# A two-piece fp32 product on TensorE: the high weight piece against two halves into one place, instead of 512 columns into two

## The chip, the cores and the metric

One core of one Trainium2 chip runs the whole program. Times are microseconds (us) of device time. The kernel before was run three times: 2857.05 us median, 2854.23 to 2864.59. The profile is of one further execution.

## The reference, cut to what matters

Two transformer blocks over 256 tokens of width 2048, in fp32. The first has a gated short convolution, a state space mixer (SSD) and attention over a memory, then latent attention (MLA); the second has a retention mixer and an MLP with squared ReLU. What matters here is that nearly all the work is products of the activations with weight matrices in fp32:

```python
h = rms_norm(x, norm0_w);  ... = h @ w_in0 ...;   x = x + y @ w_out0
h = rms_norm(x, norm1_w);  ... = h @ w_in1 ...;   x = x + y @ w_out1
q, k, v, g = split(rmsnorm(x, norm1) @ ret_w_in); ...  x = x + y @ ret_w_out
x = x + square(relu(rmsnorm(x, norm2) @ mlp_w_up)) @ mlp_w_down
return rmsnorm(x, final_norm)
```

## The kernel before, in words

Activations are kept transposed: 128 features on the partitions, T = 256 tokens along the row. To get near fp32 accuracy out of the one-pass fp32r matmul, each value is split in two fp32r pieces. For activations the pieces `m[:, 0]` (high) and `m[:, 1]` (low) lie side by side, 512 columns in all (`hs`, `ys`, `lat`). For a weight tile of 128x128, ScalarE writes the rounded high piece `w_hi` (L403) and VectorE the remainder `w_lo` (L727), eight tiles in one operation of 128x1024. The product wanted is `w_hi*m_hi + w_hi*m_lo + w_lo*m_hi`.

The program goes through phases in a fixed order (`PHASES`): mem, gate, gate_out, ssd, out0, latent, latent_tail, memq, mla, out1, ret_a, ret_out_a, ret_b, ret_out_b, then up and down four times. Each phase is a loop whose body is a row of panels. A panel is up to 16 weight tiles (1 MB of fp32), loaded by SyncE's queue into `raw`, and in most phases gives one output of 128x256. There are 7232 weight tiles in all. In gate_out a panel gives two outputs of 8 tiles each; in out0 and out1 two panels of 10 tiles give one output.

On TensorE a tile is two matmuls (`panel`, L1395 and L1398): `w_hi` against all 512 columns, into both halves of a PSUM bank of `pj`, and `w_lo` against the 256 high columns, into the first half. A bank so gathers two partial sums that have still to be added. VectorE reads only one operand from PSUM here, so ScalarE first copies the first half into `half` (L408, `copy_half`), and VectorE adds the second half to it (L736 or L739, `evac`). Where the output has to be scaled by `rstd`, a second VectorE operation follows (L741). In the phases that add to the residual stream (`residual`), the sum goes to a small tile and a further operation adds it to `xT` (L932); the up phases then need three more operations for the squared ReLU.

`pj` has two banks, so output o may only start once output o-2 has been taken (semaphore `evacuated`). `w_hi` and `w_lo` have four slots of eight tiles: the pieces of panel p+2 overwrite those of panel p, once TensorE has started on the other half of the panel (`half_started`). Each engine works through its own list in written order. On ScalarE this is, per panel j: `split` half 0 of panel j+2, `copy_half` of output j, `split` half 1. On VectorE it is the same with `evac` in the middle. What a phase adds of its own (tanh, softmax, norms) stands between these.

Three further waits will be named. `square_sum` (L1495) is the sum of squares of the new residual stream, which TensorE can only start when VectorE has added up the last output of the phase (L948 is the drain that signals it). `qk_ready` in mla (L1234) comes when VectorE has turned the rotary part, after the outputs 3 and 4 of the body. And the out phases wait for the last rows of `ys` (L748).

Of the kernel before, what the change touches and what calls it, by code (L numbers as in the profile page):

```python
# [25 lines left out]
P = 128  # L26
# [83 lines left out]
def build(nc, streams, w_dt, vecs, consts, mla_mask, ret_tab, ret_decay, pos, x, mem, out):  # L110
    ctx = ExitStack()
    with ctx:
# [14 lines left out]
        kv = sb("kv", [P, 2048])  # L127
        half = sb("half", [P, NB, T])
        wdt = sb("wdt", [P, 16, 32])
# [73 lines left out]
        output_ready = sem("output_ready")  # L203
        half_copied = sem("half_copied")
        evacuated = sem("evacuated")
# [185 lines left out]
        def _(act):  # L391
# [60 lines left out]
            def mem_body(i):  # L452
                for j in range(8):
                    split("mem", i, j, 0)
                    copy_half("mem", i, j)
                    split("mem", i, j, 1)
                    if i == 0 and j < 2:
                        act.wait_ge(S["x_rows"], 16)
                        row_square(1, rows, j)
                        if j == 1:  # L460
                            act.drain().then_inc(S["x_squares"], 1)
                    if i == 0 and j == 2:
                        row_rsqrt(1, "x_var", "x_rsqrt")
                    if i == 1 and j < 4:
                        hi_columns(16 + 2 * j, hs, "norm0")
                        hi_columns(17 + 2 * j, hs, "norm0")
                    if j >= 5:
                        value_rows(i, j - 5)
                value_rows(i, 3)
# [8 lines left out]
            def gate_body(i):  # L478
                for j in range(4):
# [3 lines left out]
                    split("gate", i, j, 0)  # L483
                    copy_half("gate", i, j)
                    split("gate", i, j, 1)
# [8 lines left out]
            def gate_out_body(i):  # L494
                for j in range(4):
                    split("gate_out", i, j, 0)
                    copy_half("gate_out", i, 2 * j)
                    copy_half("gate_out", i, 2 * j + 1)
                    split("gate_out", i, j, 1)
# [4 lines left out]
            def residual(name, ppo):  # L504
# [3 lines left out]
                def body(i):  # L508
                    for j in range(len(PHASES[name][0])):
                        split(name, i, j, 0)  # L510
                        if j % ppo == ppo - 1:
                            o = j // ppo
                            copy_half(name, i, o)
                        split(name, i, j, 1)
# [25 lines left out]
            def ssd_body(i):  # L540
                O = outputs("ssd", i)
                M = Count(0, 1, i)
                for j in range(12):
# [33 lines left out]
                    copy_half("ssd", i, j)  # L577
                    split("ssd", i, j, 1)
# [8 lines left out]
            def copy_body(name):  # L587
                def body(i):
                    for j in range(len(PHASES[name][0])):
                        split(name, i, j, 0)  # L590
                        copy_half(name, i, j)
                        split(name, i, j, 1)
# [6 lines left out]
            for j in range(3):  # L599
# [4 lines left out]
                split("latent_tail", 0, j, 0)  # L604
                copy_half("latent_tail", 0, j)
                split("latent_tail", 0, j, 1)
# [3 lines left out]
            def memq_body(i):  # L610
                O = outputs("memq", i)
                M = Count(4, 2, i)
                for j in range(4):
# [4 lines left out]
                    split("memq", i, j, 0)  # L618
                    copy_half("memq", i, j)
                    if j < 3:  # L620
# [9 lines left out]
            def mla_body(i):  # L630
                O = outputs("mla", i)
                for j in range(8):
# [17 lines left out]
                    if j == 3:  # L650
                        copy_half("mla", i, 3)
                        copy_half("mla", i, 4)
                        split("mla", i, j, 0)
                    elif j == 7:
                        copy_half("mla", i, 8, 2)
                    else:
                        copy_half("mla", i, j if j < 3 else j + 1)
                    split("mla", i, j, 1)
# [7 lines left out]
            def ret_body(name, first):  # L666
                def body(i):
                    O = outputs(name, i)
                    for j in range(12):
# [20 lines left out]
                        split(name, i, j, 0)  # L690
                        copy_half(name, i, j)
                        split(name, i, j, 1)
# [8 lines left out]
            for b in range(FF_BLOCKS):  # L701
                def up_body(i):
                    for j in range(4):
                        split(f"up{b}", i, j, 0)
                        copy_half(f"up{b}", i, j)
                        split(f"up{b}", i, j, 1)
# [10 lines left out]
        def _(dve):  # L717
# [11 lines left out]

            def evac(name, i, o, dst, weight=1, scale=None, via=None):  # L730

                c = outputs(name, i)
                dve.wait_ge(half_copied, c(o, 1))
                k = c.slot(o, NB)
                if scale is None:
                    TT(dst, pj[:, k, T:2 * T], half[:, k], ALU.add).then_inc(evacuated, weight)  # L736
                else:
                    via = dst if via is None else via
                    TT(via, pj[:, k, T:2 * T], half[:, k], ALU.add)  # L739
                    dve.drain()  # L740
                    TT(dst, via, scale, ALU.mult).then_inc(evacuated, weight)  # L741

# [165 lines left out]
            def residual(name, ppo, opp=1, x_all=None):  # L908
# [8 lines left out]
                def body(i):  # L917
                    def column(gain, o):
                        return vec[:, bass.ds(i * 4 + (VEC[gain][0] + o), 1)]
                    for j in range(len(PHASES[name][0])):  # L920
# [194 lines left out]
            def latent_body(i):  # L1115
                for j in range(4):
                    split("latent", i, j, 0)
                    evac("latent", i, j, lraw[:, i * 4 + j], scale=rstd[:, 0:T], via=(krA, krB)[j % 2])
                    split("latent", i, j, 1)
# [225 lines left out]
            inverse_rms(NORM["b_mlp"] + 1, 0, D, nv, ny, nt, rstd, b=258)  # L1345
            TT(rstd_sq, rstd, rstd, ALU.mult)
            for b in range(FF_BLOCKS):
                def up_body(i):
                    for j in range(4):
                        split(f"up{b}", i, j, 0)  # L1350
                        evac(f"up{b}", i, j, up_t[j % 2])
                        split(f"up{b}", i, j, 1)
                        dve.drain()
                        STT(out=up_t[2 + j % 2], in0=up_t[j % 2], scalar=0.0, in1=up_t[j % 2], op0=ALU.max,
                            op1=ALU.mult)
                        dve.drain()
                        TT(up_t[2 + j % 2], up_t[2 + j % 2], rstd_sq[:, 0:T], ALU.mult)
                        yy = ys[:, i * 4 + j]
# [11 lines left out]
        def _(pe):  # L1370
            mm = nc.tensor.matmul

            def panel(name, i, j, pieces, before={}):
# [10 lines left out]
                for o, moving, at, opens, closes, weight in pieces:  # L1384
# [3 lines left out]
                    for t, m in enumerate(moving):  # L1388
# [483 lines left out]
```

## Time and profile before

| | |
|---|---|
| median of the three runs | 2857.05 us |
| span of the profiled execution | 2861.9 us |
| TensorE matmul, busy | 2769.8 us (97%), 15792 matmuls and as many weight loads |
| VectorE busy | 1954.6 us (68%) |
| ScalarE busy | 1405.5 us (49%) |
| DMA | 173 GB/s in the mean, queue q1 busy 49.2% |
| granted TensorE clock | 0.986 in the mean |

The profiled execution took 2861.9 us from its first to its last instruction; this is 4.9 us above the median of the runs shown, within their spread. A matmul's start in the profile is real, its end is modelled, so matmuls overlap on the page: the time of one is read as the distance from its start to the next start. PEld is the weight load, which runs beside the matmul ahead of it. In the chain that ended last, 90% of the span is TensorE's, 56% of the span on line 1395 and 28% on line 1398.

### The profile page before, as it was taken

To read this page: it belongs to the slowest core of one execution; us is meant where nothing else is said; L and a number is where in the kernel's file an instruction comes from. 1 tells how busy PE (TensorE), PEld (TensorE's weight loads), DVE (VectorE), ACT (ScalarE), POOL (GpSimd) and SP (SyncE) were. 2 spreads that over 40 slices of the span, in tenths; PEclk is the share of its full clock that TensorE was granted. 3 is DMA by queue.
4 is the path that set the end of the run, shared out by engine and by line. 5 is a ranking of instruction groups with operands and counts; after the bars stand their busy time and mean duration, and the time that the engine had idled before them with its cause. 6 is when DMAs were issued, how large, how long until landed. Compare 5 with 4: busy or idle time off the path is not lost.

```text
span 2861.9 us, 46279 instructions
## 1 busy us (share of the span) xinstructions
PE 2769.8 (97%) x15792; PEld 2412.3 (84%) x15792; DVE 1954.6 (68%) x3079; ACT 1405.5 (49%) x2199; POOL 35.4 (1%) x56
## 2 busy tenths in 40 slices
PE   6999999999999899999999999999999999999998
PEld 5888888888888788888888888888888888888887
DVE  5566567787767777777666655666667677576775
ACT  5544245555554555556555534555554444444444
POOL 0000000000000001000000000000000000000000
PEclk9999899999999999999999999999999999999999
DMA  5555354444664334465454455454445555555553
GB/s 230 193 190 191 119 193 151 154 147 149 199 226 152 112 128 159 150 194 182 169 179 172 172 176 182 177 179 171 152 166 188 191 189 191 191 191 190 187 188 110
DMA packets 76338, 495.57 MB, mean 173 GB/s; under 512 B 8544, under 2 KB 8672, under 8 KB 23792
## 3 DMA queue, kind: packets, MB, share of 16 engines
q1 hardware_dynamic: 73568, 478.18, 49.2%
q0 software_dynamic: 2000, 13.70, 1.3%
q10 hardware_dynamic: 704, 2.83, 0.3%
q8 instruction: 38, 0.62, 0.1%
q14 instruction: 28, 0.23, 0.0%
HBM read 486.29 MB, written 8.39 MB: 173 GB/s over the span
## 4 chain that ended last, share of the span: by engine, by line
PE 90%; DVE 4%; ACT 2%; issue 2%; DVEq 1%; DMA 0%; ACTq 0%; POOLq 0%
PE pj L1395 56%; PE pj L1398 28%; PE mx L1410 1%; ACT w_hi L403 1%; PE mx L1466 1%; DVE w_lo L727 1%; PE mx L1695 0%; PE mx L1636 0%; DVEq L930 0%; PE mx L1525 0%; PE mx L1637 0%; PE mx L1687 0%; PE mx L1702 0%; DMA xT<-in_mem 0%; PE mx L1513 0%
## 5 line engine op out<-in xcount | busy, mean ns | idle before, releaser
L1395 PE MATMUL pj<-hs,w_hi 128*128 128x512 f32 x4400 | 1562.2, 399 | 6.7 <-DVE xT L741 5.0
L727 DVE TENSOR_TENSOR w_lo<-raw,w_hi 128x1024 fp32r<-128x1024 f32 x1010 | 1137.0, 1130 | 480.6 <-ACT w_hi L403 463.0
L403 ACT ACTIVATE w_hi<-raw 128x1024 fp32r<-128x1024 f32 x1010 | 983.2, 979 | 672.7 <-PE pj L1395 669.2
L1398 PE MATMUL pj<-hs,w_lo 128*128 128x256 f32 x4400 | 1231.2, 280 | 0.0
L1395 PEld LDWEIGHTS pj<-hs,w_hi 128*128 128x128 f32 x4400 | 829.0, 188 | 198.9 <-DVE xT L741 5.3
L1395 PE MATMUL pj<-ys,w_hi 128*128 128x512 f32 x2560 | 906.3, 398 | 20.3 <-DVE ys L748 14.2
L1398 PEld LDWEIGHTS pj<-hs,w_lo 128*128 128x128 f32 x4400 | 833.6, 189 | 3.7 <-issue 2.9
L1398 PE MATMUL pj<-ys,w_lo 128*128 128x256 f32 x2560 | 720.5, 281 | 0.0
L1395 PEld LDWEIGHTS pj<-ys,w_hi 128*128 128x128 f32 x2560 | 483.8, 189 | 136.0 <-DVE ys L748 15.4
L1398 PEld LDWEIGHTS pj<-ys,w_lo 128*128 128x128 f32 x2560 | 487.8, 191 | 0.0
L408 ACT ACTIVATE half<-pj 128x256 f32<-128x256 f32 x491 | 186.9, 381 | 557.5 <-PE pj L1398 556.6
L736 DVE TENSOR_TENSOR gen<-pj,half 128x256 f32<-128x256 f32 x412 | 173.7, 422 | 140.3 <-ACT half L408 134.6
L1395 PE MATMUL pj<-lat,w_hi 128*128 128x512 f32 x272 | 102.2, 415 | 3.9 <-DVE gen L736 2.5
L932 DVE TENSOR_TENSOR xT<-xT,gen 128x256 f32 (+1 forms) x144 | 61.3, 425 | 27.9 <-issue 27.5
L1398 PE MATMUL pj<-lat,w_lo 128*128 128x256 f32 x272 | 76.8, 282 | 0.0
L1395 PEld LDWEIGHTS pj<-lat,w_hi 128*128 128x128 f32 x272 | 51.8, 190 | 20.7 <-issue 5.0
L519 ACT ACTIVATE gen<-xT 128x256 f32 (+1 forms) x64 | 26.8, 418 | 61.6 <-DVE xT L932 61.5
L748 DVE TENSOR_TENSOR ys<-gen,ys 128x256 f32 (+1 forms) x88 | 42.8, 486 | 14.6 <-issue 14.6
L1398 PEld LDWEIGHTS pj<-lat,w_lo 128*128 128x128 f32 x272 | 52.2, 192 | 0.2
L739 DVE TENSOR_TENSOR gen<-pj,half 128x256 f32<-128x256 f32 x59 | 24.9, 423 | 28.1 <-ACT half L408 27.7
L1410 PE MATMUL mx<-con,xT 128*128 128x128 f32 x136 | 22.3, 319 | 21.3 <-DVE xT L785 20.7
L937 DVE TENSOR_TENSOR gen<-gen 128x256 f32<-128x256 f32 x80 | 32.3, 421 | 11.9 <-ACT gen L519 11.9
(262 smaller groups left out, 1356.4 us busy)
## 6 DMA issues: line engine op xcount, KB each, us to landing
raw<-in_w_up SPq DMA_DIRECT2D x64, 1024.0 KB, 4.8
raw<-in_w_down SPq DMA_DIRECT2D x64, 1024.0 KB, 4.8
raw<-in_w_ssd SPq DMA_DIRECT2D x48, 1024.0 KB, 4.8
raw<-in_w_ret_a SPq DMA_DIRECT2D x48, 1024.0 KB, 4.8
raw<-in_w_ret_b SPq DMA_DIRECT2D x48, 1024.0 KB, 4.8
raw<-in_w_out SPq DMA_DIRECT2D x64, 640.0 KB, 3.9
raw<-in_w_gate SPq DMA_DIRECT2D x32, 1024.0 KB, 4.8
raw<-in_w_mem SPq DMA_DIRECT2D x16, 1024.0 KB, 5.0
```

Of the source, the lines that this page charges most:

```text
L403: A(w_hi[:, s, 0:b - a, :], raw[:, c.slot(p, 4), a:b, :], ACT.Copy).then_inc(hi_ready, 1)
L408: A(half[:, c.slot(o, NB)], pj[:, c.slot(o, NB), 0:T], ACT.Copy).then_inc(half_copied, weight)
L519: ins = A(sq[k][o % 2], xT[:, i * 4 + o], ACT.Square, scale=dyn(gain, i, o))
L727: TT(w_lo[:, s, 0:b - a, :], raw[:, c.slot(p, 4), a:b, :], w_hi[:, s, 0:b - a, :].bitcast(F32), ALU.subtract).then_inc(split_ready, 1)
L736: TT(dst, pj[:, k, T:2 * T], half[:, k], ALU.add).then_inc(evacuated, weight)
L748: return TT(dst[1], src, dst[0].bitcast(F32), ALU.subtract)
L932: TT(xo, xo, res[(o + u) % 2], ALU.add).then_inc(S["x_tile"], 1)
L937: TT(acc[k], acc[k], sq[k][o % 2], ALU.add)
L1395: ins = mm(pj[:, k], w_hi[:, s + h, u], m, start=opens and t == 0, stop=False)
L1398: ins = mm(pj[:, k, 0:T], w_lo[:, s + h, u], m[:, 0], start=False, stop=closes and t == len(moving) - 1)
L1410: return nc.tensor.transpose(dst, src, ident)
L1466: ins = mm(mx[:, 0, 32 * r:32 * r + 32], hs[:, k, part, 128 * r:128 * r + 128].bitcast(F32), wdt[:, k], start=k == 0 and part == 0, stop=k ...
```

## The change

A tile is now three matmuls of 256 columns, all into the first half of the bank: `w_hi` against the high columns, `w_hi` against the low columns, `w_lo` against the high columns. PSUM then holds the finished sum. `copy_half` becomes `panel_done`: ScalarE still waits for the output at the same place in its list, and copies nothing. VectorE takes the output in one operation that reads PSUM: a copy (plain outputs), a multiplication by `rstd` (scaled outputs), an addition into `xT` (residual phases), or `max(.,0) * rstd` (up phases). The tile `half` and its semaphore are gone.

```diff
-            def copy_half(name, i, o, weight=1):
-                c = outputs(name, i)
-                act.wait_ge(output_ready, c(o, 1))
-                A(half[:, c.slot(o, NB)], pj[:, c.slot(o, NB), 0:T], ACT.Copy).then_inc(half_copied, weight)
+            def panel_done(name, i, o):
+                act.wait_ge(output_ready, outputs(name, i)(o, 1))
...
-            def evac(name, i, o, dst, weight=1, scale=None, via=None):
+            def product(name, i, o):
                 c = outputs(name, i)
-                dve.wait_ge(half_copied, c(o, 1))
-                k = c.slot(o, NB)
+                dve.wait_ge(output_ready, c(o, 1))
+                return pj[:, c.slot(o, NB), 0:T]
+
+            def evac(name, i, o, dst, weight=1, scale=None):
+                src = product(name, i, o)
                 if scale is None:
-                    TT(dst, pj[:, k, T:2 * T], half[:, k], ALU.add).then_inc(evacuated, weight)
+                    v.tensor_copy(dst, src).then_inc(evacuated, weight)
                 else:
-                    via = dst if via is None else via
-                    TT(via, pj[:, k, T:2 * T], half[:, k], ALU.add)
-                    dve.drain()
-                    TT(dst, via, scale, ALU.mult).then_inc(evacuated, weight)
+                    TT(dst, src, scale, ALU.mult).then_inc(evacuated, weight)
...
                             for u in range(opp):
-                                if u:
-                                    dve.drain()
-                                evac(name, i, o + u, res[(o + u) % 2])
-                                dve.drain()
                                 xo = xT[:, i * n_out + (o + u)]
-                                TT(xo, xo, res[(o + u) % 2], ALU.add).then_inc(S["x_tile"], 1)
+                                TT(xo, xo, product(name, i, o + u), ALU.add).then_inc(evacuated, 1)
+                                dve.drain().then_inc(S["x_tile"], 1)
...
-            TT(rstd_sq, rstd, rstd, ALU.mult)
...
-                        evac(f"up{b}", i, j, up_t[j % 2])
+                        STT(out=up_t[j % 2], in0=product(f"up{b}", i, j), scalar=0.0, in1=rstd[:, 0:T], op0=ALU.max,
+                            op1=ALU.mult).then_inc(evacuated, 1)
                         split(f"up{b}", i, j, 1)
                         dve.drain()
-                        STT(out=up_t[2 + j % 2], in0=up_t[j % 2], scalar=0.0, in1=up_t[j % 2], op0=ALU.max,
-                            op1=ALU.mult)
-                        dve.drain()
-                        TT(up_t[2 + j % 2], up_t[2 + j % 2], rstd_sq[:, 0:T], ALU.mult)
+                        TT(up_t[2 + j % 2], up_t[j % 2], up_t[j % 2], ALU.mult)
...
-                        ins = mm(pj[:, k], w_hi[:, s + h, u], m, start=opens and t == 0, stop=False)
+                        ins = mm(pj[:, k, 0:T], w_hi[:, s + h, u], m[:, 0], start=opens and t == 0, stop=False)
                         if u == 0:
                             ins.then_inc(half_started, 1 if h else started)
+                        mm(pj[:, k, 0:T], w_hi[:, s + h, u], m[:, 1], start=False, stop=False)
                         ins = mm(pj[:, k, 0:T], w_lo[:, s + h, u], m[:, 0], start=False,
                                  stop=closes and t == len(moving) - 1)
```

TensorE's list in the mla body of before, at the border from the last tile on `lat` to the first panel on `hs`, two tiles of it. The waits stand behind the instruction that has them.

```order
L1398 MATMUL pj<-lat,w_lo 128x256
L1641 REGISTER_ALU
L1410 MATMUL mx<-con,gen 128x128 [waits evacuated]
L1410 MATMUL mx<-con,gen 128x128
L1383 REGISTER_ALU
L1395 MATMUL pj<-hs,w_hi 128x512 [waits evacuated,weights_split_ready]
L1398 MATMUL pj<-hs,w_lo 128x256
```

The same place now:

```order
L1391 MATMUL pj<-lat,w_lo 128x256
L1634 REGISTER_ALU
L1403 MATMUL mx<-con,gen 128x128 [waits evacuated]
L1403 MATMUL mx<-con,gen 128x128
L1375 REGISTER_ALU
L1387 MATMUL pj<-hs,w_hi 128x256 [waits evacuated,weights_split_ready]
L1390 MATMUL pj<-hs,w_hi 128x256
L1391 MATMUL pj<-hs,w_lo 128x256
```

The waits stand where they stood; a tile is three rows instead of two.

VectorE's list of before at the end of the last down phase (the last split, then the last output of all, its part in the sum of squares and its final gain):

```order
L727 TENSOR_TENSOR w_lo<-raw,w_hi 128x1024 [waits weights_hi_ready]
L937 TENSOR_TENSOR gen<-gen 128x256 [waits x_square]
L944 TENSOR_SCALAR xT<-xT,vec 128x256
L736 TENSOR_TENSOR gen<-pj,half 128x256 [waits half_copied]
L932 TENSOR_TENSOR xT<-xT,gen 128x256
L937 TENSOR_TENSOR gen<-gen 128x256 [waits x_square]
```

The same place now:

```order
L724 TENSOR_TENSOR w_lo<-raw,w_hi 128x1024 [waits weights_hi_ready]
L932 TENSOR_TENSOR gen<-gen 128x256 [waits x_square]
L939 TENSOR_SCALAR xT<-xT,vec 128x256
L926 TENSOR_TENSOR xT<-xT,pj 128x256 [waits output_ready]
L932 TENSOR_TENSOR gen<-gen 128x256 [waits x_square]
```

The operation that read `half` is gone, and the addition into `xT` itself waits for TensorE's output.

## Rows read from the trace of the kernel before

**Rows 1.** The page, span and busy time of each engine.
```profile
span 2861.9 us, 46279 instructions
PE 2769.8 (97%) x15792; PEld 2412.3 (84%) x15792; DVE 1954.6 (68%) x3079; ACT 1405.5 (49%) x2199; POOL 35.4 (1%) x56
```
**Rows 2.** Stretches, matmuls into pj alone: window, length, PE busy (matmuls), clock.
```profile
150.00:300.00 150.00, 150.00 (x868) 1.00 0.55 190
725.00:825.00 100.00, 100.00 (x568) 1.00 0.68 215
2140.00:2840.00 700.00, 700.00 (x4041) 1.00 0.53 183
```
**Rows 3.** Waits of TensorE: engine, line, releaser: us, times, longest.
```profile
PE mx L1495 <- DVEq L948: 16.1, 4, 5.2
PE pj L1395 <- DVE ys L748: 14.2, 4, 4.8
PE mx L1636 <- DVEq L1234: 9.5, 8, 1.3
PE pj L1395 <- DVE xT L741: 5.0, 1, 5.0
PE mx L1513 <- ACT xT L626: 4.9, 2, 2.5
```
**Rows 4.** Timeline of TensorE in an up phase: start, duration, engine, line.
```profile
2200.03 0.39 PE L1395 MATMUL pj<-hs,w_hi 128*128 128x512 f32 x1
2200.26 0.28 PE L1398 MATMUL pj<-hs,w_lo 128*128 128x256 f32 x1
2200.38 0.39 PE L1395 MATMUL pj<-hs,w_hi 128*128 128x512 f32 x1
```
**Rows 5.** Chain of 311 to 315 us: start, us, piece; matmuls of 32 columns.
```profile
310.89 4.13 PE mx L1466 x37
```
**Rows 6.** TensorE at half clock, in ret_out_b, behind a wait.
```profile
2041.93 0.63 PE L1395 MATMUL pj<-ys,w_hi 128*128 128x512 f32 x1
2042.36 0.41 PE L1398 MATMUL pj<-ys,w_lo 128*128 128x256 f32 x1
2042.57 0.63 PE L1395 MATMUL pj<-ys,w_hi 128*128 128x512 f32 x1
```
**Rows 7.** The page, costliest groups: the copies; out<-in, count, busy, mean ns, idle before.
```profile
L408 ACT ACTIVATE half<-pj 128x256 f32<-128x256 f32 x491 | 186.9, 381 | 557.5 <-PE pj L1398 556.6
```
**Rows 8.** Timeline behind the last output of all, 2845.6 to 2848.4 us.
```profile
2845.72 0.38 ACT L408 ACTIVATE half<-pj 128x256 f32<-128x256 f32 x1 [3.73 <-PE pj L1398]
2846.14 0.42 DVE L736 TENSOR_TENSOR gen<-pj,half 128x256 f32<-128x256 f32 x1 [3.43 <-ACT half L408]
2846.66 0.42 DVE L932 TENSOR_TENSOR xT<-xT,gen 128x256 f32<-128x256 f32 x1
...
2848.35 0.37 PE L1495 MATMUL mx<-con,gen 128*128 128x1 f32 x1 [2.67 <-DVEq L948]
```
**Rows 9.** Timeline in mla, 1017 to 1020 us: outputs 3, 4 and the rotary part.
```profile
1017.12 0.38 ACT L408 ACTIVATE half<-pj 128x256 f32<-128x256 f32 x1 [1.00 <-PE pj L1398]
1017.40 1.70 ACT L403 ACTIVATE w_hi<-raw 128x256 fp32r<-128x256 f32 x3
...
1019.75 0.49 PE L1636 MATMUL mx<-gen 128*128 128x128 f32 x2 [1.28 <-DVEq L1234]
```
**Rows 10.** Timeline in latent_tail and memq: a scaled output on VectorE.
```profile
938.47 0.42 DVE L739 TENSOR_TENSOR xT<-pj,half 128x256 f32<-128x256 f32 x1
938.96 0.42 DVE L741 TENSOR_TENSOR xT<-xT,wdt 128x256 f32<-128x256 f32 x1
```
**Rows 11.** Timeline in gate_out, 350.3 to 357.5 us.
```profile
350.82 1.06 ACT L403 ACTIVATE w_hi<-raw 128x1024 fp32r<-128x1024 f32 x1 [2.19 <-PE pj L1395]
...
353.53 0.51 PE L1395 MATMUL pj<-ys,w_hi 128*128 128x512 f32 x1 [0.16 <-DVE gen L736]
```
**Rows 12.** The page, DMA queue that fetches TensorE's instructions: packets, MB, share.
```profile
q8 instruction: 38, 0.62, 0.1%
```

More of the change, by code:

```diff
@@ L127, in build @@
         kv = sb("kv", [P, 2048])
-        half = sb("half", [P, NB, T])
         wdt = sb("wdt", [P, 16, 32])
@@ L203, in build @@
         output_ready = sem("output_ready")
-        half_copied = sem("half_copied")
         evacuated = sem("evacuated")
@@ L454, in mem_body @@
                     split("mem", i, j, 0)
-                    copy_half("mem", i, j)
+                    panel_done("mem", i, j)
                     split("mem", i, j, 1)
@@ L483, in gate_body @@
                     split("gate", i, j, 0)
-                    copy_half("gate", i, j)
+                    panel_done("gate", i, j)
                     split("gate", i, j, 1)
@@ L496, in gate_out_body @@
                     split("gate_out", i, j, 0)
-                    copy_half("gate_out", i, 2 * j)
-                    copy_half("gate_out", i, 2 * j + 1)
+                    panel_done("gate_out", i, 2 * j)
+                    panel_done("gate_out", i, 2 * j + 1)
                     split("gate_out", i, j, 1)
@@ L512, in body @@
                             o = j // ppo
-                            copy_half(name, i, o)
+                            panel_done(name, i, o)
                         split(name, i, j, 1)
@@ L576, in ssd_body @@
                         A(th[j % 2], cv[j % 2], ACT.Tanh).then_inc(S["conv_tanh"], 1)
-                    copy_half("ssd", i, j)
+                    panel_done("ssd", i, j)
                     split("ssd", i, j, 1)
@@ L590, in body @@
                         split(name, i, j, 0)
-                        copy_half(name, i, j)
+                        panel_done(name, i, j)
                         split(name, i, j, 1)
@@ L604, in _ @@
                 split("latent_tail", 0, j, 0)
-                copy_half("latent_tail", 0, j)
+                panel_done("latent_tail", 0, j)
                 split("latent_tail", 0, j, 1)
@@ L618, in memq_body @@
                     split("memq", i, j, 0)
-                    copy_half("memq", i, j)
+                    panel_done("memq", i, j)
                     if j < 3:
@@ L650, in mla_body @@
                     if j == 3:
-                        copy_half("mla", i, 3)
-                        copy_half("mla", i, 4)
+                        panel_done("mla", i, 3)
+                        panel_done("mla", i, 4)
                         split("mla", i, j, 0)
                     elif j == 7:
-                        copy_half("mla", i, 8, 2)
+                        panel_done("mla", i, 8)
                     else:
-                        copy_half("mla", i, j if j < 3 else j + 1)
+                        panel_done("mla", i, j if j < 3 else j + 1)
                     split("mla", i, j, 1)
@@ L690, in body @@
                         split(name, i, j, 0)
-                        copy_half(name, i, j)
+                        panel_done(name, i, j)
                         split(name, i, j, 1)
@@ L704, in up_body @@
                         split(f"up{b}", i, j, 0)
-                        copy_half(f"up{b}", i, j)
+                        panel_done(f"up{b}", i, j)
                         split(f"up{b}", i, j, 1)
@@ L1117, in latent_body @@
                     split("latent", i, j, 0)
-                    evac("latent", i, j, lraw[:, i * 4 + j], scale=rstd[:, 0:T], via=(krA, krB)[j % 2])
+                    evac("latent", i, j, lraw[:, i * 4 + j], scale=rstd[:, 0:T])
                     split("latent", i, j, 1)
```

## The prediction, as put on record before the changed kernel ran

> **What bounds the kernel now.** I read the page's busy times first. TensorE is busy 2769.8 of 2861.9 us [rows 1], but a modelled end says little, so the next view is the stretches. In the long run of up and down phases, 700 us hold 4041 matmuls into `pj`, two to a tile, without a gap: 0.3465 us a tile [rows 2]. All 7232 tiles at that pace are 2506 us. TensorE's own pace is the bound, and the other engines matter only where TensorE waits for them. Of those waits the large ones are few [rows 3]: 16.1 us before four sums of squares, 14.2 us before four out phases, 9.5 us in mla, 5.0 and 4.9 us in latent and memq. The change adds to the first quantity and takes from the second. So I need two things: what the third matmul costs, 7232 times, and which waits have `half` or the second VectorE operation in their chain.
>
> **The third matmul.** In the up phase a 512-column matmul is followed after 0.23 us, and a 256-column one after 0.12 us [rows 4]; with the tile at 0.3465 that is 0.1165 for 256 columns. The two high matmuls of 256 columns replace one of 512. If each takes what the low one takes now, a tile is 3 x 0.1165 = 0.3495 us, 3.0 ns more than now. Every matmul in this profile has its own weight load (15792 of each, [rows 1]), so `w_hi` will be loaded twice, and the new load has only 0.1165 us of matmul to hide behind. But so has the load of `w_hi` now, behind the 256 columns of `w_lo`: the 0.1165 already holds a load. What a load alone needs is seen where 32-column matmuls stand in a row: 37 in 4.13 us, 0.112 each [rows 5]. It fits, with 5 ns to spare. At half clock (1.2 GHz) the distances are 0.43 and 0.21 us [rows 6], so twice 256 is 512 and the split is free there.
>
> The pace is not the same everywhere. The first phases have 868 matmuls in 150 us (0.3456 a tile), out0 568 in 100 us (0.3521) [rows 2]. I have no row for what 256 columns take in the slower stretches that is finer than 0.01 us, and take 0.3495 for all. The sum by phases, tiles counted from the panel table:
> mem, gate, ret_out_b, up and down: 3072 tiles, +3.0 ns, +9.2 us;
> out0, out1, ret_out_a: 896 tiles, 0.3495 for 0.3521, -2.3 us;
> ssd, latent, memq, mla, retention: 3136 tiles, taken in the middle of the two paces (0.3493), +0.6 us;
> gate_out: 128 tiles, not bound by this (below), 0.
> Together +7.5 us.
>
> The bounds. From below, the second high matmul, whose weights are already there, could follow at the load's own pace, 0.112 us: -4.7 ns a tile, -34 us. If all three ran at 0.112, a tile were 0.336: -98 us, the lowest that a row here allows. From above: the same tile takes 0.3521 in out0 against 0.3465 in up, so something not on the page can add 5.6 ns. If the new matmul met it each time, that is +40 us. I take 0.1165, the row that has this very matmul with this very load.
>
> By the Trainium skill (TensorE: Matmul & The Clock Gate, Back-to-back issue gap) a warm matmul of N columns costs N/2.4 + 2.5 ns alone. The trace disagrees in size: by that rule a tile is 325 ns, the rows have 346.5. In its difference it agrees, since one matmul more is +2.5 ns a tile, +18 us over all tiles, and with the savings below the sum would be 2868 us.
>
> **What the shorter way out of PSUM saves.** 491 copies by ScalarE go, 186.9 us of its time [rows 7], and about as many VectorE operations in the scaled, residual and up phases. Most save nothing: in up and down TensorE never waits, with `pj` double-buffered and a panel of 5.5 us against a few tenths. ScalarE's wait stays in its list where the copy was, so its later work moves up by the copy only. What counts is five kinds of places.
>
> Behind the last output of all, the chain is copy at 2845.72, addition at 2846.14, addition into `xT` at 2846.66, and TensorE at 2848.35 [rows 8]. The last addition now starts where the copy does: 0.9 us. (Its signal comes by a drain behind it, a little later.)
>
> The three other sums of squares (16.1 us of waits in all, [rows 3]) have a split of 1.2 us on VectorE in the chain; it waits for ScalarE's high piece, which starts one copy later than it could. In mla the copy starts at 1017.12 and the next `w_hi` at 1017.40 [rows 9]: 0.28 us each, and somewhat more where VectorE is the late one. 3 x 0.35 = 1.0 us.
>
> Scaled outputs take two operations 0.49 us apart [rows 10] and will take one. This stands in the chain of TensorE's waits in memq (two), latent (one) and before the two retention out phases [rows 3]. 5 x 0.49 = 2.5 us. At the start of out0 the last output is not scaled, so nothing.
>
> In mla, TensorE waits 1.28 us at 1019.75 [rows 9] for the rotary part, once in each of eight passes, behind output 4, a split, and two operations. The split comes 0.28 us sooner: 8 x 0.28 = 2.2 us.
>
> In gate_out the ring is: second half started, `w_hi` at 350.82, then `w_lo`, the output taken, and TensorE at 353.53 [rows 11]. VectorE does its split before it takes the output, so the copy was hidden behind it and its removal gives nothing here; the addition into `xT` replaces an equal operation. But the signal that the half has started hangs on the first high matmul, which now ends after 256 columns, 0.11 us sooner. 8 x 0.11 = 0.9 us.
>
> Sum of the savings: 0.9 + 1.0 + 2.5 + 2.2 + 0.9 = 7.5 us. Nothing may hide (0), or, as VectorE's list is shorter everywhere and some chains hold two outputs, it may be double (15). Where a stall goes, the next is late: in the retention ends the norm's own chain on VectorE, which stays.
>
> **The sum.** 2861.9 + 7.5 - 7.5 = 2861.9 for the profiled execution. The two terms cancel, so against the runs shown I forecast their median, 2857.
>
> **Rivals.**
> A, the forecast: every 256-column matmul follows after about 0.1165 us. 2857, with 2846 to 2871 as its own range (savings 0 to 15, pace within 1 ns a tile).
> B: the second matmul on the same weights is cheaper. One of three at 0.112 gives 2857 - 34 = 2823. For it: there is slack in [rows 5]. Against: the low matmul does not get that pace with a load of its own in steady phases.
> C, the other side, slower than before: the third weight load per tile meets what slows out0. Place: each tile of the 6300 on the faster paces. Price: 5.6 ns beyond A each, 2857 + 35 = 2892; it decides from about 2 ns, where the loss passes the 0.5%. For it: loads now fill nearly all of TensorE's time (3 x 0.112 = 0.336 of 0.3495 us, against 0.224 of 0.3465), and nothing in this profile ever ran fp32r tiles so tightly for long. Against: the load behind `w_lo` is as tight now, and keeps the pace.
> D, also slower: the loop bodies outgrow what TensorE keeps of its instructions. An ssd or retention body has 192 tiles, 768 matmuls and loads now, 1152 then. 38 packets fetched 0.62 MB [rows 12] for 31584 executed instructions [rows 1], so bodies are replayed and not fetched again. If the longer ones were, 12 passes would each wait for at least one packet; the queue's share, 0.1% of 16 engines, makes 1.2 us of one. 12 x 1.2 x 1 to 5 packets is 14 to 72 us: 2871 to 2929. Nothing on the page shows the store's size. By the Trainium skill (Runtime: NRT & Kernel Launch, Instruction fetch mechanics) TensorE's store holds 2048 instructions, so the body would fit and this rival be void, while its warning that a taken branch out of the current pages forces a fetch would hit now as then; the 38 packets speak against that warning.
> E: the change doesn't pay on the way out, because ScalarE still stops at each output. Then the third matmul stands alone: 2864.5.
>
> **How the numbers follow.** 0.5% of 2857 is 14 us, about what a measurement can tell here. A has 0.50, B 0.20, C 0.18, D 0.05, E 0.07. Faster by over 14 us: B nearly whole and the lower edge of A, where savings double and the slower phases lose their extra: 0.19 + 0.07 = 0.26. Slower: C 0.16, D 0.05, the upper edges of A and E 0.05, in all 0.26. Within: 0.48. The range of 8 in 10 runs from just below B to just above C: 2820 to 2896; the extremes (three at 0.112, D with several packets) are left out.
>
> **What would show it.** In the up and down phases the stretch of 700 us should hold three matmuls per 0.3495 us, some 6009 of them; distances between starts 0.11 to 0.12 for all three lines. Less than 6009 by over 1% is C, more is B. TensorE's wait behind the last output should fall from 2.67 to about 1.8 us, the eight in mla from 9.5 to about 7.3 us in all. ScalarE should lose 187 us of busy time and VectorE some 100 to 200, without TensorE's idle time changing by more than 15 us. Packets of q8 should grow to some 56; far more means D. I am wrong if the tile's pace differs by over 2 ns from 0.3495, in either direction.

## The result, and the profile after

The changed kernel takes 2918.23 us (median of 4 runs, 2916.35 to 2920.37); before took 2858.33 beside it (4 runs, 2854.23 to 2864.59). The ratio is 1.0197, interval 1.017 to 1.0223: 60 us slower, outside the range of the prediction. The profiled execution has a span of 2917.4 us against 2861.9.

The page of the kernel after, its first lines (against [rows 1]), the queue that fetches instructions (against [rows 12]), and the groups that took the place of [rows 7] and L932:

```profile
span 2917.4 us, 60302 instructions
PE 2837.6 (97%) x23024; PEld 2807.2 (96%) x23024; DVE 1854.8 (64%) x2803; ACT 1267.4 (43%) x1708; POOL 37.0 (1%) x56
...
q8 instruction: 54, 0.88, 0.1%
...
L737 DVE COPY gen<-pj 128x256 f32<-128x256 f32 x204 | 85.9, 421 | 43.6 <-PE pj L1391 43.0
L926 DVE TENSOR_TENSOR xT<-xT,pj 128x256 f32 (+1 forms) x144 | 60.3, 419 | 64.6 <-PE pj L1391 64.2
```

There are 7232 matmuls more, one for each tile, and weight loads now fill 96% of the span. ScalarE and VectorE are less busy, and TensorE's share is the same 97%. VectorE's operations on an output cost what they cost before, 0.42 us.

Stretches of the kernel after, matmuls into `pj` alone (window, length, PE busy with their count, clock, DMA share, GB/s), against [rows 2]:

```profile
150.00:300.00 150.00, 150.00 (x1252) 1.00 0.53 182
2200.00:2800.00 600.00, 600.00 (x5003) 1.00 0.53 183
```

A window counts the two or three matmuls that reach into it from its start. 5000 in 600 us are 0.1200 us each, 0.3600 a tile; the first stretch gives the same (1249 in 150 us, 0.1201). The prediction had 0.3495.

TensorE in a down phase of the kernel after (start, duration, engine, line), against [rows 4]:

```profile
2299.83 0.28 PE L1387 MATMUL pj<-ys,w_hi 128*128 128x256 f32 x1
2299.95 0.28 PE L1390 MATMUL pj<-ys,w_hi 128*128 128x256 f32 x1
2300.07 0.28 PE L1391 MATMUL pj<-ys,w_lo 128*128 128x256 f32 x1
2300.19 0.28 PE L1387 MATMUL pj<-ys,w_hi 128*128 128x256 f32 x1
```

All three distances are 0.12 us, the repeated weights included. In [rows 4] they were 0.23 and 0.12 by the rounded stamps.

Waits of TensorE in the kernel after (line, releaser: us in total, times, longest), against [rows 3]:

```profile
PE mx L1488 <- DVEq L943: 14.1, 4, 4.7
PE pj L1387 <- DVE ys L746: 11.9, 4, 3.8
PE mx L1629 <- DVEq L1229: 9.3, 8, 1.3
...
PE pj L1387 <- DVE xT L739: 3.7, 1, 3.7
PE mx L1506 <- ACT xT L623: 3.0, 2, 1.5
PE pj L1387 <- DVE gen L737: 2.3, 1, 2.3
```

The five waits of [rows 3] have gone from 49.7 to 42.0 us. The sum of all the waits listed falls from 86.3 to 73.2.

The memq phase as a window, before and then after (the two phase borders differ; length, PE busy with all its matmuls, clock):

```profile
905.40:973.10 67.70, 57.81 (x306) 0.92 0.24 76
```
```profile
922.70:986.40 63.70, 56.95 (x434) 0.97 0.25 81
```

This phase is 4 us shorter in spite of its slower tiles. Both the 5.0 and the 4.9 us of [rows 3] lie in it, and they are 3.7 and 3.0 us now: shorter waits account for 3.2 us. The granted clock in it rose from 0.92 to 0.97, since less of it ran at 1.2 GHz after its waits.

**Where the 55.5 us come from.** The tile's pace: 3072 tiles in mem, gate, ret_out_b, up and down went from 0.3466 to 0.3600 us (+41), 896 in out0, out1 and ret_out_a from 0.3533 (+6), 3136 elsewhere from the middle of the two paces, 0.350 (+31): together some +78 us. Against this stand some -23 us: 13 from shorter waits, about 5 from less time at half clock (an estimate: the whole span's mean clock is 0.986 before and 0.988 after, 0.2% of 2900 us), and some 5 us that I can't assign to single places.

### The profile page after: what moved, and what is told of

It reads as the page before. It is cut to its first block, busy times and chain, and to the rows that moved or that the text cites. A ratio compares the mean times of both kernels' runs of the same rounds, so it can differ in the third digit from the quotient of the medians.

```text
span 2917.4 us, 60302 instructions
## 1 busy us (share of the span) xinstructions
PE 2837.6 (97%) x23024; PEld 2807.2 (96%) x23024; DVE 1854.8 (64%) x2803; ACT 1267.4 (43%) x1708; POOL 37.0 (1%) x56
## 4 chain that ended last, share of the span: by engine, by line
PE 86%; issue 7%; DVE 3%; ACT 1%; DVEq 1%; POOL 1%; DMA 1%; ACTq 0%; POOLq 0%
PE pj L1387 27%; PE pj L1390 27%; PE pj L1391 27%; PE mx L1459 1%; PE mx L1403 1%; ACT w_hi L401 1%; POOL gen L372 1%; PE mx L1688 0%; PE mx L1518 0%; PE mx L1680 0%; PE mx L1695 0%; DVE w_lo L724 0%; DMA xT<-in_mem 0%; PE mx L1525 0%; PE mx L1506 0%
## 5 line engine op out<-in xcount | busy, mean ns | idle before, releaser
L1387 PE MATMUL pj<-hs,w_hi 128*128 128x256 f32 x4400 | 1264.4, 287 | 5.1 <-DVE xT L739 3.7
L1390 PE MATMUL pj<-hs,w_hi 128*128 128x256 f32 x4400 | 1247.8, 284 | 0.0
L1391 PE MATMUL pj<-hs,w_lo 128*128 128x256 f32 x4400 | 1247.7, 284 | 0.0
L1387 PEld LDWEIGHTS pj<-hs,w_hi 128*128 128x128 f32 x4400 | 847.1, 193 | 9.2 <-DVE xT L739 3.9
L1390 PEld LDWEIGHTS pj<-hs,w_hi 128*128 128x128 f32 x4400 | 847.5, 193 | 3.8 <-issue 2.9
L1391 PEld LDWEIGHTS pj<-hs,w_lo 128*128 128x128 f32 x4400 | 847.0, 193 | 0.0
L1387 PE MATMUL pj<-ys,w_hi 128*128 128x256 f32 x2560 | 731.3, 286 | 16.1 <-DVE ys L746 11.9
L1390 PE MATMUL pj<-ys,w_hi 128*128 128x256 f32 x2560 | 728.1, 284 | 0.0
L1387 PEld LDWEIGHTS pj<-ys,w_hi 128*128 128x128 f32 x2560 | 495.3, 193 | 18.6 <-DVE ys L746 12.7
L1390 PEld LDWEIGHTS pj<-ys,w_hi 128*128 128x128 f32 x2560 | 495.5, 194 | 0.0
L737 DVE COPY gen<-pj 128x256 f32<-128x256 f32 x204 | 85.9, 421 | 43.6 <-PE pj L1391 43.0
L926 DVE TENSOR_TENSOR xT<-xT,pj 128x256 f32 (+1 forms) x144 | 60.3, 419 | 64.6 <-PE pj L1391 64.2
L1387 PE MATMUL pj<-lat,w_hi 128*128 128x256 f32 x272 | 80.0, 294 | 2.3 <-DVE gen L737 2.3
L1390 PE MATMUL pj<-lat,w_hi 128*128 128x256 f32 x272 | 77.6, 285 | 0.0
L1387 PEld LDWEIGHTS pj<-lat,w_hi 128*128 128x128 f32 x272 | 52.8, 194 | 2.7 <-issue 2.5
L1390 PEld LDWEIGHTS pj<-lat,w_hi 128*128 128x128 f32 x272 | 52.9, 194 | 0.2
```

The source lines that it names most:

```text
L737: v.tensor_copy(dst, src).then_inc(evacuated, weight)
L926: TT(xo, xo, product(name, i, o + u), ALU.add).then_inc(evacuated, 1)
L1387: ins = mm(pj[:, k, 0:T], w_hi[:, s + h, u], m[:, 0], start=opens and t == 0, stop=False)
L1390: mm(pj[:, k, 0:T], w_hi[:, s + h, u], m[:, 1], start=False, stop=False)
```

## The experiments

T below is the theory that I formed from the two traces: an fp32r matmul that loads its own weights costs its columns at 2.4 GHz and 13.3 ns beside. Two such are 320 + 26.7 = 346.7 ns, three are 360. Ratios are against the kernel before on the same chip, whose median lay between 2863 and 2870 us there.

**The split matmul, into two halves, with the old way out.** Before, with L1395 split:

```diff
-ins = mm(pj[:, k], w_hi[:, s + h, u], m, ...)
+ins = mm(pj[:, k, 0:T], w_hi[:, s + h, u], m[:, 0], ...)
+mm(pj[:, k, T:2 * T], w_hi[:, s + h, u], m[:, 1], start=False, stop=False)
```

> The kernel before with only its 512-column matmul split in two of 256, still into the two halves of the bank, and the old way out (copy, addition). Theory T (each fp32r matmul costs its columns at 2.4 GHz plus a fixed 13.3 ns, whatever its place and its neighbours): 0.360 us a tile in every phase, about 80 us more than before, 2938 us, none of the savings on the way out. Rival P (the place: three matmuls in a row into the same 256 addresses hold each other up): 0.3495 to 0.350 a tile and about 2865 us. Rival L (a weight load needs 120 ns when no longer matmul covers it): 0.360 like T.

2931.24 us (2928.99 to 2933.74), ratio 1.021 (1.0191 to 1.0229). Stretches of it:

```profile
150.00:300.00 150.00, 150.00 (x1252) 1.00 0.52 182
...
2200.00:2700.00 500.00, 500.00 (x4169) 1.00 0.52 183
```

4166 in 500 us are 0.1200 each, 0.360 a tile. Where the products land makes no difference; the third matmul costs the whole of it. Its span is 2927.5 us, 65.6 more than before's, where the pace alone makes 78: some 12 us are given back with the old way out. TensorE's listed waits are 78.5 us here against 86.3, and the mean clock is 0.988 against 0.986. Tiles that last longer hide more of what ScalarE and VectorE have to do.

**The way out alone.** The kernel after with before's two matmuls, so `w_hi*m_lo` lands in the second half and is never added:

```diff
-ins = mm(pj[:, k, 0:T], w_hi[:, s + h, u], m[:, 0], ...)
-mm(pj[:, k, 0:T], w_hi[:, s + h, u], m[:, 1], start=False, stop=False)
+ins = mm(pj[:, k], w_hi[:, s + h, u], m, ...)
```

> The matmuls of before (512 and 256 columns), with the new way out: one VectorE operation from the first half, no copy. The part w_hi*m_lo, which lies in the second half, is left out of the result. If the time outside the tile's pace in the changed kernel (25 us less than before, by phases) is all the way out: pace as before (0.3467 and 0.3533 by phase) and 2833 us. Rival (my own sum of the savings): 2851 us.

2841.27 us (2838.05 to 2856.64), ratio 0.989 (0.9872 to 0.9907): 29 us less by the medians, between the two outcomes that I had named. That isn't the way out alone, though: executions of this kernel and of before have two paces (below), and each median takes them as they fell. Its waits:

```profile
PE mx L1487 <- DVEq L943: 14.3, 4, 4.8
PE pj L1387 <- DVE ys L746: 11.1, 3, 4.2
PE mx L1628 <- DVEq L1229: 9.7, 8, 1.3
PE pj L1387 <- DVE xT L739: 3.9, 1, 3.9
```

They shrink as in the kernel after. Its long stretch, in the profiled execution:

```profile
2200.00:2700.00 500.00, 500.00 (x2832) 1.00 0.53 187
```

That is 0.3533 us a tile, the slower of before's two paces, which no part of the edit touches; more on this below. The profiled span is 2855.1 us, 6.8 less than before's, though some 2000 tiles of up and down ran 6.7 ns slower than in before's profile (+13), while the 256 of ret_out_a ran as much faster (-2). So the way out gave some 18 us here, more than twice the 7.5 us that I had added up. TensorE's listed waits fell by 11 us of this (86.3 to 75.3), and the mean clock rose from 0.986 to 0.988.

**Other widths.** The kernel after with 128 columns in each matmul (except the first tile of an output), half of the products left out; and with 320, overlapping:

```diff
-m[:, 0] ... m[:, 1]
+mf[:, 0:128] ... mf[:, 256:384]      (first kernel)
+mf[:, 0:320] ... mf[:, 192:512]      (second kernel)
```

> The changed kernel with each of the three matmuls of a tile cut to 128 columns (the first tile of each output excepted); half of the columns of every product are left out. T: 53.3 + 13.3 = 67 ns of matmul, so the load is the bound, at the 0.112 us of the 32-column matmuls: 0.336 a tile. Rival L: the load needs 120 ns in any case, so 0.360 a tile, unchanged though half of the columns are gone.

> The changed kernel with each of the three matmuls at 320 columns (the extra 64 overlap what the others have; the result is not the reference's). T: 133.3 + 13.3 = 146.7 ns each, 0.440 a tile. Rival L: 320 columns cover a load of 120 ns, so only the columns and the 2.5 ns of a plain fp32 matmul stay: 136 ns each, 0.408 a tile. Rival C (cost in proportion to the columns, 0.443 ns each plus 3 ns, as the two distances of before suggested): 145 ns each, 0.435.

128 columns: 3804.9 us (one execution), far slower with half the columns. An early stretch at full clock, and one late:

```profile
210.00:290.00 80.00, 80.00 (x717) 1.00 0.55 194
3000.00:3100.00 100.00, 100.00 (x471) 0.50 0.30 105
```

At 2.4 GHz a matmul of 128 columns takes 80/714 = 0.112 us, less than the 0.120 of 256 columns: so 0.120 isn't what a load needs, and 0.112 is, as in [rows 5]. Later the granted clock is 0.50 (1.2 GHz), at about 0.21 us each, although TensorE is busy all the time. The clock of this kernel in 40 slices of its span:

```profile
PEclk8996699955579998699656996555555555555555
```

So only its early stretch tells something of the load; its total is a matter of the clock.

320 columns: 3465.68 us (one execution). TensorE in it:

```profile
2599.95 0.31 PE L1396 MATMUL pj<-hs,w_lo 128*128 128x320 f32 x1
2600.10 0.31 PE L1392 MATMUL pj<-hs,w_hi 128*128 128x320 f32 x1
...
2600.98 0.31 PE L1392 MATMUL pj<-hs,w_hi 128*128 128x320 f32 x1
```

Six matmuls from 2600.10 to 2600.98: 0.147 each, where L had 0.136 and C 0.145. 320 columns at 2.4 GHz are 0.1333, so 13.3 to 13.7 ns stand beside them again. They don't grow with the columns, nor shrink with the cover that a longer matmul gives the next load.

**The low weight against 512 columns.** Before with

```diff
-ins = mm(pj[:, k, 0:T], w_lo[:, s + h, u], m[:, 0], ...)
+ins = mm(pj[:, k], w_lo[:, s + h, u], m, ...)
```

> The kernel before, with the low weight also taken against all 512 columns (both halves), so a tile is two matmuls of 512; w_lo*m_lo is then added, which the reference's sum of three products leaves out. Theory T (columns at 2.4 GHz plus 13.3 ns for every matmul): 213.3 + 13.3 = 226.7 ns between all starts, 453.3 ns a tile, so +107 ns over 7,232 tiles: about +770 us, 3,620 to 3,640 us. Rival S (the start distances of the kernel before are what they look like: 230 after a 512-column matmul): 460 ns a tile, some 3,680 us. Rival C (one cost for a tile, 26.7 ns whatever the number of matmuls): gives the same 453.3 here as T and isn't told apart by this run.

3581.86 us (one execution). TensorE in it:

```profile
1000.03 0.39 PE L1395 MATMUL pj<-ys,w_hi 128*128 128x512 f32 x1
1000.25 0.39 PE L1398 MATMUL pj<-ys,w_lo 128*128 128x512 f32 x1
...
1001.39 0.39 PE L1395 MATMUL pj<-ys,w_hi 128*128 128x512 f32 x1
```

Six distances in 1.36 us: 0.2267, T's value, not 0.230. The 230 and 116.5 that I had read as the prices of two matmuls are an uneven split of the same 346.7. The total is 40 to 60 us below T's, since I had counted no wait as hidden by the longer tiles (argued, not tested by itself).

**Half the weight columns.** The kernel after, but in all tiles but the first and last of an output:

```diff
-w_hi[:, s + h, u], w_lo[:, s + h, u]   -> pj[:, k, 0:T]
+w_hi[:, s + h, u, 0:64], w_lo[:, s + h, u, 0:64]   -> pj[0:64, k, 0:T]
```

> The changed kernel with only 64 of the 128 weight columns in each matmul, except in the first and the last tile of an output: half of the output rows of the other tiles are left out, the moving columns stay 256. Theory T with its 13.3 ns fixed for each matmul: 120.0 ns between starts as before, time as the changed kernel's, 2,900 to 2,930 us. Rival G (the 13.3 ns is a piece of the weight load that shows, and goes by its size): 113 to 114 ns between starts, about 20 ns less a tile, 2,760 to 2,800 us. If the clock falls for lack of activity, the distances at full clock are what counts.

2802.96 us (one execution), just above G's range and far from T's. TensorE in it:

```profile
2299.84 0.28 PE L1396 MATMUL pj<-hs,w_lo 128*64 128x256 f32 x1
2299.95 0.28 PE L1392 MATMUL pj<-hs,w_hi 128*64 128x256 f32 x1
...
2300.86 0.28 PE L1396 MATMUL pj<-hs,w_lo 128*64 128x256 f32 x1
```

Nine in 1.02 us: 0.1133 each, 6.7 ns beside the columns. Here T as I had put it, with a fixed 13.3 ns, fails, and G's distances are right: the price is halved with the weight columns, by these two sizes 0.104 ns for each. That it is a part of the load which isn't hidden is my reading and not shown: the edit halves the load and, with it, the output rows of each matmul, and no run tells the two apart.

**The order in a tile.** The kernel after with high-by-high, low-by-high, high-by-low:

```diff
-mm(..., w_hi, m[:, 1]); ins = mm(..., w_lo, m[:, 0])
+mm(..., w_lo, m[:, 0]); ins = mm(..., w_hi, m[:, 1])
```

> The changed kernel with the three matmuls of a tile in the order high-by-high, low-by-high, high-by-low, so that no two matmuls that follow each other inside a tile load the same weights. Theory T (every matmul loads its own weights and pays 13.3 ns whatever was there): 120.0 ns between all starts, 2,910 to 2,925 us. Rival R (a repeated load is cheaper or dearer than a new one and the 120.0 is a mean by the queue): the distance after the second matmul changes by over 1 ns, the tile by as much.

2920.44 us (one execution). TensorE in a down phase of it:

```profile
2299.80 0.28 PE L1387 MATMUL pj<-ys,w_hi 128*128 128x256 f32 x1
2299.92 0.28 PE L1390 MATMUL pj<-ys,w_lo 128*128 128x256 f32 x1
2300.04 0.28 PE L1391 MATMUL pj<-ys,w_hi 128*128 128x256 f32 x1
2300.16 0.28 PE L1387 MATMUL pj<-ys,w_hi 128*128 128x256 f32 x1
```

Every distance is 0.12 us, as in the kernel after.

A load of weights that are there already is neither cheaper nor dearer. Rival B of the prediction had no ground.

**Three matmuls only where something waits.** Before, with a function `one` that picks memq, gate_out, mla's outputs but 7, output 3 of ret_out_b and the last output of all; about 740 tiles:

```diff
+if one(name, i, o):
+    ins = mm(pj[:, k, 0:T], w_hi[:, s + h, u], m[:, 0], ...)
+    mm(pj[:, k, 0:T], w_hi[:, s + h, u], m[:, 1], ...)
+else:
     ins = mm(pj[:, k], w_hi[:, s + h, u], m, ...)
```

> The kernel before, with the three-matmul tile and the one-operation way out only for the outputs that something waits for: all of memq, gate_out and mla (but output 7 of mla), output 3 of ret_out_b, and the last output of the last down block; about 700 of the 7,232 tiles. Theory T (each fp32r matmul costs its columns at full rate plus 13.3 ns, so a tile of three costs 13.3 ns more than a tile of two): these tiles cost about 0.0133 x 700 = +9 us at most, and less where they sit in phases that ran at 353.3 ns; the phase sums of the changed kernel gave back memq 5.2, mla 7.2, ret_out_b 2.5, gate_out 1.6 and about 1 at the last output, net of their pace, some 17.5 us in all; the net of these is about -10 us against before (ratio near 0.9965). Rival W (the savings come only where all outputs before them are taken in one operation too, since ScalarE's copies of the other outputs still stand in its queue): no net gain, ratio 1.000 to 1.003.

2864.61 us (2850.11 to 2872.63, 12 runs), ratio 0.9978 (0.9954 to 1.0002). The interval takes in 1, so a gain isn't shown, and neither T's 0.9965 nor W's 1.000 is ruled out. The runs spread over 22 us, which those of the kernel after don't (4 us).

**The kernel before once more.**

> The kernel before, unchanged, profiled once more. Question: is the slower of its two paces (353.3 ns a tile against 346.7, in out0, latent, out1 and ret_out_a of the first profile) tied to those phases, or to the execution? Theory F (phases: what is loaded or how long the panels are): the same phases at 353.3 here. Rival X (the execution: a state in which a loop is entered): another set of phases at 353.3, and a span that goes with their number of tiles, 6.7 us for each 1,000 tiles.

2876.81 us, span 2875.3. The same stretches in the first execution of before, and in this one:

```profile
150.00:300.00 150.00, 150.00 (x868) 1.00 0.55 190
733.00:833.00 100.00, 97.87 (x555) 1.00 0.67 205
2200.00:2700.00 500.00, 500.00 (x2887) 1.00 0.55 189
```
```profile
150.00:300.00 150.00, 150.00 (x851) 1.00 0.53 185
733.00:833.00 100.00, 98.65 (x570) 1.00 0.68 215
2200.00:2700.00 500.00, 500.00 (x2832) 1.00 0.54 185
```

The first and the long stretch now have 0.3534 us a tile where they had 0.3466, and out0 (the middle one) has 0.347 us of busy time a tile where it had 0.353: the other way round. By X, some 2560 slower tiles and 300 faster ones make 15 us; the spans differ by 13.4. So X holds in the main: a phase isn't bound to a pace, which is settled anew in each execution, and this makes a large part of the spread of before's runs. Not every phase changed: out1 had the slower pace in both profiles (512 and 511 matmuls in 90 us), and ret_out_a too (399 and 398 in 70 us), but in the profile of the way out alone ret_out_a had the faster one (405).

**Turned order.** Before, with every second tile low first:

```diff
-ins = high(); ...; ins = low()
+one_, two_ = (low, high) if t % 2 else (high, low)
+ins = one_(); ...; ins = two_()
```

> The kernel before with the two matmuls of every second tile in turned order: high, low, low, high, so a 512-column matmul follows another 512 and a 256 another 256. Theory T (columns at 2.4 GHz plus 13.3 ns for every matmul, in any order): two tiles are 693.3 ns, as before in its faster phases: 226.7 between the two high ones, 120.0 between the two low ones. For the slower pace there are two guesses. Theory Y (it comes from the change of length, 512 behind 256, and costs 6.7 ns each time): a slow phase has 350 a tile at most. Rival Z (it needs the strict alternation of 512 and 256, and is gone with it): 346.7 in every phase, and with it the spread of the runs; then about 7 to 20 us faster than before, ratio 0.993 to 0.998. If the order doesn't matter at all: ratio 1.000.

2864.6 us (2859.47 to 2865.96, 10 runs), ratio 0.9985 (0.9967 to 1.0003). Its long stretch:

```profile
2200.00:2700.00 500.00, 500.00 (x2873) 1.00 0.55 189
```

2871 in 500 us are 0.3483 a tile, and the other phases have the same where nothing waits. The pace is single now, neither 346.7 nor 353.3, so neither Y (at most 350) nor Z is quite what happened, though Y's bound holds. The interval takes in 1, so it isn't shown to be faster. The spread fell from 19 us (before, beside it) to 6.5, and what is left goes with the clock: nine runs with a mean clock of 0.983 or 0.984 took 2863.5 to 2866.0 us, the one with 0.986 took 2859.5.

**Both together.** The turned order, with `one` as above.

> Both findings put together: two-matmul tiles in turned order (high, low, low, high) everywhere, and the three-matmul tile with the one-operation way out only for memq, gate_out, the mla outputs but 7, output 3 of ret_out_b and the last output of the last down block. Theory T with the pace of the turned kernel (348.1 ns a tile instead of 346.7 or 353.3 by chance): the turned order gave ratio 0.9985, the phases of the first hybrid gave back about 5 us of 2,862 in memq, gate_out and mla, so 0.9965, about 10 us faster than before, with a spread of the runs of some 7 us instead of 20. Rival: the two don't add, because the turned order delays the first half_started or the end of an output, ratio 0.9985 or above.

2854.67 us (2853.84 to 2856.66, 12 runs), ratio 0.9961 (0.9944 to 0.9977): 9 us faster than before by the medians, 11 by the ratio, as forecast. By its median it is the fastest kernel here that computes all three products, and its runs lie within 3 us. Its waits in memq and before the sums of squares:

```profile
PE mx L1533 <- DVEq L971: 15.0, 4, 5.2
...
PE pj L1427 <- DVE xT L746: 4.1, 1, 4.1
...
PE mx L1551 <- ACT xT L633: 3.0, 2, 1.5
```

The last was 4.9 in [rows 3]. Not tried was one load for two matmuls, which would take away what the split costs: an fp32r matmul brings its own load in every trace here.

## Why the prediction was wrong

**The failed step** is "if each takes what the low one takes now, a tile is 3 x 0.1165 = 0.3495 us". The sum of a tile, 0.3465, was read rightly. Its split was not: I took the distance behind the 512-column matmul (0.23) as its price and gave the remainder to the low one. With 512 behind 512 the distance is 0.2267, with 256 behind 256 it is 0.1200; alternating, the low one starts 3 ns late, and 0.1165 is what is left over, no price of a matmul. What each matmul of 128 weight columns adds is its columns and 13.3 ns: the pair has 26.7, three have 40. The mis-sized term is +3.0 ns a tile predicted, +13.4 measured in the fast stretches; +7.5 us predicted over all, some +78 measured. The columns are the same on both sides, and that was the clue: 0.3465 less 768 columns at 2.4 GHz (0.320) leaves 0.0265 for two matmuls, and half of that for a third gives 0.3598.

**The bounds** failed with it. The 5.6 ns taken as the most from above came from the difference between two paces, and no run ties that to a third load. The row that should have made an upper bound was there: two matmuls, 26.5 ns of overhead. The half-clock rows ([rows 6]) were rightly read but bear only on a few us. Two smaller slips: 0.3456 and 0.3521 count the matmuls that reach into a window, and without them are 0.3464 and 0.3533; one matmul at 0.112 instead of 0.1165 saves 4.5 ns a tile and 33 us, not 4.7 and 34.

**Rival C** had the right side and place (each tile, the third load) but neither mechanism nor size: 8.6 ns a tile against 13.4. Its sentence "it decides from about 2 ns" held. B, D and E fell: B by the turned pair of products (no cheaper load), D by 54 packets where 56 were foreseen, E by the second experiment.

By the Trainium skill (TensorE: Matmul & The Clock Gate, Back-to-back issue gap) a warm matmul of 256 columns alone would cost 109.2 ns; the page itself says that at small N this counts too little, having no budget for the weight load. The rows have 120.0 with 128 weight columns and 113.3 with 64. I had taken its difference (+2.5 ns a matmul) for a confirmation after seeing that its size was wrong by 21 ns a tile; those 21 ns were the price that was missing, 10.8 ns at each of two matmuls.

**The savings** were of the right kind, and too small. Item by item, the wait behind the last output, of the kernel after from 2880 us on:

```profile
PE mx L1488 <- DVEq L943: 1.8, 1, 1.8
```

It was 2.67 and was to be 1.8. The four sums of squares fell by 2.0 (forecast 1.9 with the last). The scaled outputs: ys 2.3, memq 3.2 (the wait that I had put in latent stands in memq, at 922 us), together 5.5 against 2.5. At the five places that I had counted, TensorE waits 19.5 us before, 18.2 with the longer tiles alone (first experiment), 15.6 with the way out alone (second) and 14.2 with both. So 1.3 us come from the longer tiles and 3.9 from the way out. I had counted the second operation alone; a chain of two outputs saves ScalarE's copy as well, which I take for the rest without having tested it. In mla I expected 9.5 to become 7.3 and it is 9.3. What took its place is seen on VectorE of the kernel after, behind output 4:

```profile
1030.67 0.42 DVE L724 TENSOR_TENSOR w_lo<-raw,w_hi 128x256 fp32r<-128x256 f32 x1 [0.18 <-ACT w_hi L401]
1031.72 0.42 DVE L1226 TENSOR_TENSOR gen<-gen 128x256 f32<-128x256 f32 x1 [0.63 <-POOL gen L372]
1032.22 0.42 DVE L1228 TENSOR_TENSOR gen<-gen 128x256 f32<-128x256 f32 x1
1032.73 0.49 PE L1629 MATMUL mx<-gen 128*128 128x128 f32 x2 [1.26 <-DVEq L1229]
```

VectorE is early and now waits 0.63 us for GpSimd's part of the rotation, which I had not put on the path. The trace of before had it there, nearly as late:

```profile
1015.34 3.22 POOL L374 TENSOR_TENSOR gen<-gen 32x256 f32<-32x256 f32 x4 [27.37 <-DVE gen L736]
1018.76 0.41 DVE L1231 TENSOR_TENSOR gen<-gen 128x256 f32<-128x256 f32 x1
```

GpSimd ends at 1018.56, only 0.20 us ahead of VectorE's operation. Then two effects that I left out: less time at half clock behind shorter waits (about 5 us), and longer tiles, which hide more (the 12 us of the first experiment). So the savings of the parts don't add: 12 and 18 us in the traces apart, 23 together.

**The other expectations.** ScalarE lost 138 us of busy time, not 187: the copies overlapped the next operation by 0.1 us (in [rows 9] the copy runs to 1017.50 and `w_hi` starts at 1017.40), 491 times. VectorE lost 100, the lower edge of what was said. The count of matmuls in the long stretch was to be 6009 in 700 us, or 5150 in 600; it is 5003.

## What to carry to other kernels

Price a matmul from a total: the time of a period, less its columns at the granted clock, divided by the number of loads in it. Never take the distance between two starts as the price of one of them. Splitting a wide matmul in two costs that remainder once more each time (13.3 ns here); that is worth it only at the few outputs that somebody waits for.

## What the runs showed of the hardware

- An fp32r matmul with its own load of 128 weight columns took N columns at 2.4 GHz and 13.3 to 13.7 ns: 120.0 for 256, 147 for 320, 226.7 for 512. With 64 weight columns (and so 64 output rows) it took 113.3 for 256. With 128 moving columns it took 112 ns, the same as with 32, so there the columns are not the bound.
- Strict alternation of 512 and 256 columns had two paces, 346.7 and 353.3 ns a tile. In some phases they changed places between executions, and two such executions differed by 13.4 us. Equal widths had one pace; turned order (512, 256, 256, 512) had 348.3. What picks the pace stays open.
- With 128 moving columns the granted clock went down to 0.50 and stayed there for the last 15 of 40 slices of the span, with TensorE busy throughout; with 256 and more it was 0.98 to 1.00 in the long stretches.
- Longer loop bodies were not fetched again: 54 packets for 46048 matmuls and weight loads executed. By the Trainium skill (Runtime: NRT & Kernel Launch, Instruction fetch mechanics) a taken branch out of the current pages forces a fetch; the packets show nothing of it here.
